# Moving the head norms, the ropes and the convolutions of a decoder layer in among the input projections

## The reference, cut to what matters

```python
h = _rmsnorm(x, P['norm1_w']) * (1.0 + sc1) + sh1
proj = jnp.einsum('btd,de->bte', h, P['w_in'])
q, kv, nsa_gate, dn_qkv, dn_a, dn_b, dn_z, merge = _split_cols(proj, IN_SPLITS)
q = _rope(_rmsnorm(q.reshape(B, T, NSA_HEADS, HEAD_DIM), P['q_norm_w']), pos)
kc = _rmsnorm(kc, P['k_norm_w'][0])
ksl = _rope(_rmsnorm(ksl, P['k_norm_w'][1]), pos)
kw = _rope(_rmsnorm(kw, P['k_norm_w'][2]), pos)
...
y = xx[:, 0:T] * P['dn_conv_w'][0]
for j in range(1, DN_CONV):
    y = y + xx[:, j:j + T] * P['dn_conv_w'][j]
y = jax.nn.silu(y)
```

## Time and profile before

| | us |
|---|---|
| median of 3 runs | 3313.51 |
| lowest and highest run | 3309.18 and 3320.33 |
| the profiled execution | 3319.12 |
| span of its trace | 3317.3 |
| TensorE busy | 2925.8 (88% of the span) |
| VectorE busy | 1695.2 (51%) |
| ScalarE busy | 965.3 (29%) |

### The profile page before, as it was taken

The page is one execution under the profiler, slowest core; times in us unless marked ns, Lnnn a source line. Parts: engine busy times, 40 slices in busy tenths (PEclk is TensorE's granted clock), DMA queues, the critical chain, the costliest instruction groups (busy, mean ns, idle before and its releaser), DMA issues.

```text
span 3317.3 us, 42568 instructions
## 1 busy us (share of the span) xinstructions
PE 2925.8 (88%) x16456; PEld 2463.2 (74%) x16456; DVE 1695.2 (51%) x2731; ACT 965.3 (29%) x1257; POOL 18.6 (1%) x21
## 2 busy tenths in 40 slices
PE   5799895684467879989889999999999999999999
PEld 2577773563256848879888888888887888888887
DVE  0154425551253150046535987777674666666665
ACT  1000001241121111123331135554443444444443
POOL 0000000000000000000000000000000000000000
PEclk8899997796678779989999999999999999999999
DMA  9565676113312036665433445566697788887885
GB/s 399 219 228 208 231 292 208 56 47 102 147 76 83 32 149 256 253 278 194 164 129 145 172 171 222 217 229 221 263 391 288 253 293 284 295 288 283 291 284 184
DMA packets 182494, 707.03 MB, mean 213 GB/s; under 512 B 20854, under 2 KB 119798, under 8 KB 144758
## 3 DMA queue, kind: packets, MB, share of 16 engines
q1 hardware_dynamic: 170726, 671.94, 54.7%
q10 hardware_dynamic: 9360, 16.85, 1.3%
q0 software_dynamic: 2304, 16.78, 1.3%
HBM read 662.81 MB, written 51.09 MB: 215 GB/s over the span
## 4 chain that ended last, share of the span: by engine, by line
PE 79%; DVE 10%; DMA 6%; SPq 2%; issue 2%; ACT 2%; DVEq 0%; ACTq 0%
PE psum L554 13%; PE psum L1039 12%; PE psum L1088 7%; PE psum L1090 7%; PE psum L1089 7%; PE psum L1040 6%; PE psum L998 5%; PE psum L914 3%; PE psum L915 3%; PE psum L916 3%; DMA ring<-in_w_ada 3%; PE psum L534 2%; PE psum L1019 2%; DMA ring<-in_w_in 1%; DVE xT L1572 1%
## 5 line engine op out<-in xcount | busy, mean ns | idle before, releaser
L554 PE MATMUL psum<-hT,ring 128*128 128x264 f32 x2560 | 602.4, 398 | 70.5 <-DMA ring<-in_w_in 33.6
L1995 DVE TENSOR_TENSOR w_lo<-ring,w_hi 128x1024 fp32r<-128x1024 f32 x464 | 545.0, 1219 | 196.5 <-ACT w_hi L1449 196.5
L554 PEld LDWEIGHTS psum<-hT,ring 128*128 128x128 f32 x2560 | 499.2, 196 | 168.8 <-issue 69.1
L1039 PE MATMUL psum<-h_both,w_hi 128*128 128x512 f32 x1664 | 593.1, 399 | 1.2 <-DVE h_both L2011 1.2
L1040 PE MATMUL psum<-h_both,w_lo 128*128 128x256 f32 x1664 | 466.0, 280 | 0.0
L1449 ACT ACTIVATE w_hi<-ring 128x1024 fp32r<-128x1024 f32 x464 | 451.9, 1045 | 32.8 <-ACT CK L1436 25.6
L1088 PE MATMUL psum<-w_hi,acts 128*128 128x512 f32 x1024 | 398.6, 389 | 0.5 <-DVE acts L2047 0.5
L1090 PE MATMUL psum<-w_hi,acts 128*128 128x512 f32 x1024 | 398.4, 389 | 0.0
L1089 PE MATMUL psum<-w_lo,acts 128*128 128x512 f32 x1024 | 398.4, 389 | 0.0
L1039 PEld LDWEIGHTS psum<-h_both,w_hi 128*128 128x128 f32 x1664 | 312.7, 188 | 79.4 <-issue 7.9
L1040 PEld LDWEIGHTS psum<-h_both,w_lo 128*128 128x128 f32 x1664 | 313.1, 188 | 0.0
(11 more groups left out here) (413 smaller groups left out, 3584.5 us busy)
## 6 DMA issues: line engine op xcount, KB each, us to landing
ring<-in_w_peer_u SPq DMA_DIRECT2D x64, 2048.0 KB, 8.7
ring<-in_w_peer_v SPq DMA_DIRECT2D x64, 2048.0 KB, 7.9
ring<-in_w_ada SPq DMA_DIRECT2D x48, 2048.0 KB, 12.2
ring<-in_w_in SPq DMA_DIRECT2D x42, 2048.0 KB, 8.0
arena<-gelu_scratch SPq DMA_DIRECT2D x64, 512.0 KB, 8.6
arena<-route_w SPq DMA_DIRECT2D x64, 512.0 KB, 9.4
ring<-in_cache_cmp SPq DMA_DIRECT2D x64, 256.0 KB, 3.4
ring<-in_cache_slc SPq DMA_DIRECT2D x64, 256.0 KB, 3.0
```

The costliest lines, as they stand in the source:

```text
L554: mm = pe.matmul(bank[b + j][:, 0:NT], w[:, k, j * P:(j + 1) * P], hT[:, k, :], start=(k == 0), stop=(k == KT - 1))
L1039: pe.matmul(out, top[:, k, c], h2_both[:, :, k, 0:SEQ], start=k == 0, stop=False)
L1995: dve.tensor_tensor(w_lo[:, s, cols], ring[:, s, cols], w_hi[:, s % 2, cols], ALU.subtract).then_inc(S["expert_lo"], 1)
```

## The change

The heads' norms and ropes and most convolutions are issued within the loops of stages 1 and 2, in places written out by hand; iterations 5 to 7 of stage 1 and all of stage 2 are unrolled for it. A place is 4 x iteration + j, where j is 0 and 1 ahead of the two tiles of slot 0 and 2 and 3 ahead of those of slot 2 on TensorE, and on VectorE the point behind each of the four big instructions of a cache's compression. The sums of squares of all 14 normed heads land in 14 rows of one bank (a one-column selector shifts each to its row); root and reciprocal are taken once, of 14x264; a product with a 14x128 selector spreads one row over 128 partitions again, and VectorE multiplies from PSUM. On VectorE `ada_bias` moves from ahead of the cache's compression to behind it. Constants grow by 27 columns. The other numbers of the head semaphores shift.

```diff
# TensorE
+            def head_sums():
+                pe.wait_ge(S["head_act"], 1)
+                for m in range(N_HEAD):
+                    mm = pe.matmul(bank[7][0:N_HEAD, 0:NT], cst("onecol")[:, 13 - m:13 - m + N_HEAD], hsq[:, m, :],
+                                   start=(m == 0), stop=(m == N_HEAD - 1))
+                mm.then_inc(S["head_pe"], 1)
+            def head_scales(n):
+                pe.wait_ge(S["head_dve"], n + 1)
+                for j in range(2):
+                    m = 2 * n + j
+                    mm = pe.matmul(bank[4 + 3 * j][:, 0:NT], ident[0:N_HEAD, m:m + 1].broadcast_to((N_HEAD, P)), hrow,
+                                   start=True, stop=True)
+                mm.then_inc(S["head_pe"], 1)
+            def head_turn(n):
+                pe.wait_ge(S["head_dve"], n + 8)
+                for j in range(2):
+                    mm = pe.matmul(bank[4 + 3 * j][:, 0:NT], cst("perm"), PR[:, ROPE_PAIRS[n] + j, :], start=True, stop=True)
+                mm.then_inc(S["head_pe"], 1)
+            def compressed_turn():
+                pe.wait_ge(S["head_dve"], 14)
+                pe.wait_ge(S["cmp_ready"], 1)
+                pe.wait_ge(S["ada_done"], 29)
...
+            def head_step(place):
+                if place == 5 * 4 + 1:
+                    head_sums()
+                if 6 * 4 <= place < 6 * 4 + 7:
+                    head_scales(place - 6 * 4)
+                if 7 * 4 + 3 <= place < 7 * 4 + 3 + 6:
+                    head_turn(place - 7 * 4 - 3)
+                if place == 10 * 4:
+                    compressed_turn()
...
+            for i in range(3):
+                first_part(i + 8, lambda j: head_step(4 * i + 32 + j))
+                if i == 2:
+                    pe.wait_ge(S["cmp_done"], 1)
                 ada_reduce(1, 2 * i + 24)
                 ada_main(3, i + 12, 8)
                 ada_reduce(3, 2 * i + 25)
...
# ScalarE
+            def convolved(n):
+                tiles = slice(T_DNQ + 4 * n, T_DNQ + 4 * n + 4)
+                act.wait_ge(S["proj_evac"], T_DNQ + 4 * n + 8)
...
+                for b in range(4):
+                    act.wait_ge(S["conv_done"], 4 * n + b + 1)
+                    act.activation(PR[:, T_DNQ + 4 * n + b, 0:SEQ], convt[:, b, 0:SEQ], ACT.Silu).then_inc(S["conv_silu"], 1)
...
+            first_part(5, head_root)
+            first_part(6)
+            first_part(7)
+            for i in range(3):
+                first_part(i + 8, lambda j: convolved(2 * i + j) if 2 * i + j < 5 else None)
                 ada_copy(3, i + 12)
...
# VectorE
-            with dve.Fori(0, 8) as i:
-                ada_bias(i + 16, 2 * i + 32)
+            def cache_part(i, beside=lambda j: None):
                 dve.wait_ge(cache_full[3], 16 * PAGES * (i + 1))
...
+                        beside(3)
+                ada_bias(i + 16, 2 * i + 32)
...
+            def head_pair(n):
+                t0, w = HEAD_PAIRS[n]
+                dve.wait_ge(S["head_pe"], n + 2)
+                for j in range(2):
+                    ins = dve.scalar_tensor_tensor(PR[:, t0 + j, :], PR[:, t0 + j, :], par("hw")[:, w:w + 1], bank[4 + 3 * j][:, 0:NT],
+                                                   ALU.mult, ALU.mult)
+                ins.then_inc(S["head_dve"], 1)
...
+            def head_step(place):
+                if place == 5 * 4 + 2:
+                    head_rows()
+                if 6 * 4 <= place < 6 * 4 + 7:
+                    head_pair(place - 6 * 4)
+                if 7 * 4 + 3 <= place < 7 * 4 + 3 + 6:
+                    rope_pair(place - 7 * 4 - 3)
...
+            with dve.Fori(0, 5) as i:
+                cache_part(i)
+            for i in range(5, 8):
+                cache_part(i, lambda j: head_step(4 * i + j))
+            for j in range(4):
+                convolve(2 * j)
+                convolve(2 * j + 1)
+                head_step(32 + j)
+            for m in (24, 25):
+                ada_bias(m, 2 * m)
+            head_step(36)
...
+            for t in range(8, 16):
+                convolve(t)
+            for m in (26, 27):
+                ada_bias(m, 2 * m)
...
+            for t in range(16, 20):
+                convolve(t)
+            for m in (28, 29):
+                ada_bias(m, 2 * m)
+            for t in range(20, DNT):
+                convolve(t)
# SyncE
-            sp.wait_ge(S["raw_saved"], 1)
-            sp.wait_ge(S["hist_new"], 1)
+            sp.wait_ge(S["raw_saved"], 6)
+            sp.wait_ge(S["hist_new"], 6)
```

More of the change, by code:

```diff
@@ L551, in project @@
                 for j in range(2):
+                    beside(j)
                     pe.wait_ge(S["proj_evac"], t + j + 1)
@@ new lines, in head_turn @@
+            def head_turn(n):
[7 more added lines that the diff above has]
+                pe.wait_ge(S["ada_done"], 29)
+                ck = CK[:, 0, :, :, 1:1 + N_CMP].rearrange("p b g n -> p (b g) n")
+                for m in range(2):
+                    pe.matmul(bank[4 + 3 * m][:, 0:8 * N_CMP], cst("perm"), ck[:, 8 * m:8 * m + 8, :], start=True, stop=True)
+                pe.matmul(bank[6][:, 64:64 + G * N_CMP_P], cst("perm"), CP[:, 0, :, :].rearrange("p g n -> p (g n)"),
+                          start=True, stop=True).then_inc(S["cmp_rot"], 1)
@@ L578, in _ @@
+            with pe.Fori(0, 5) as i:
+                first_part(i, lambda j: None)
                 ada_reduce(1, i + 16)
[L579 to L582, removed]
+            for i in range(5, 8):
+                first_part(i, lambda j: head_step(4 * i + j))
+                ada_reduce(1, i + 16)
+            for i in range(3):
+                first_part(i + 8, lambda j: head_step(4 * i + 32 + j))
+                if i == 2:
+                    pe.wait_ge(S["cmp_done"], 1)
@@ new lines, in _, with head_root @@
+            with act.Fori(0, 5) as i:
+                first_part(i)
+            act.wait_ge(S["proj_evac"], T_DNQ + 4)
+            for n, (t0, count) in enumerate(HEAD_GROUPS):
+                m = 0 if n == 0 else 6 + 2 * n
+                ins = act.activation(hsq[:, m:m + count, :], PR[:, t0:t0 + count, :], ACT.Square)
+            ins.then_inc(S["head_act"], 1)
+            def head_root(j):
+                if j == 0:
+                    act.wait_ge(S["head_pe"], 1)
+                    act.activation(hrow, bank[7][0:N_HEAD, 0:NT], ACT.Sqrt, bias=epst[0:N_HEAD, :],
+                                   scale=1.0 / P).then_inc(S["head_act"], 1)
@@ L1181, in _ @@
[L1181 to L1196, removed]
+            convolved(5)
             act.wait_ge(S["conv_done"], DNT + 1)
@@ L1595, in head_norm, with head_rows @@
                                          ALU.mult).then_inc(S["hn_done"], 1)
[L1597 to L1608, removed]
+            def head_rows():
+                dve.wait_ge(S["head_act"], 2)
+                dve.reciprocal(hrow, hrow).then_inc(S["head_dve"], 1)
@@ new lines, in head_pair, with rope_pair @@
+            def head_pair(n):
[5 more added lines that the diff above has]
+                ins.then_inc(S["head_dve"], 1)
+            def rope_pair(n):
+                t0 = ROPE_PAIRS[n]
+                x, t = PR[:, t0:t0 + 2, :], rtmp[:, 0:2, :]
+                dve.wait_ge(S["head_pe"], n + 9)
+                dve.wait_ge(S["head_dve"], n + 8)
+                for j in range(2):
+                    dve.tensor_tensor(t[:, j, :], bank[4 + 3 * j][:, 0:NT], cst("sin"), ALU.mult)
+                step(dve.tensor_tensor(x, x, cst("cos").unsqueeze(1).broadcast_to((P, 2, NT)), ALU.mult))
+                dve.tensor_tensor(x, x, t, ALU.add).then_inc(S["head_dve"], 1)
@@ L1610, in _ @@
+            with dve.Fori(0, 5) as i:
+                cache_part(i)
+            for i in range(5, 8):
+                cache_part(i, lambda j: head_step(4 * i + j))
[6 more added lines that the diff above has]
+            head_step(36)
+            dve.wait_ge(S["head_dve"], 14)
             for v, w in enumerate(("wck", "wcv")):
```

124 lines of the change are left out of this document (56 added, 68 removed).

## The result

The changed kernel takes **3240.06 us** (median of 4 runs, 3230.76 to 3246.44); beside it on the same chip the kernel before took 3312.71 (3309.18 to 3320.33). The ratio is 0.9774, with a 95% interval of 0.9752 to 0.9796: faster by 2.3%. The forecast was 3235, with a range of 3206 to 3265. The profiled execution took 3244.72 us, with a span of 3242.9.

The account below looks back on a forecast made before the run. TensorE was taken to bound stage 2, with stages 1, 3 and 4 bound by something else. Terms +8.3 + 5.7 - 63.0 - 29.7 = -78.7 us gave 3235 us for the median; 3206 to 3265 holds 8 in 10.

Parts of the forecast that it names:

- The moved `ada_bias`: Stage 1: compression starts when its pages land, w_in is no longer late, eight iterations of products take 247.2 us.
- rival B: Stage 1, iterations 0 to 4: w_in stays late behind the pages, 23.8 us more, 3259 us; chance 0.14.
- Head products: Stage 1 on TensorE: 14 sums 6.3, 14 spreads 6.3 and one turn 0.9, together 13.5 us.
- The new waits: Stage 1, places 25 and 29 (iterations 6 and 7): TensorE waits for VectorE's pair, 11.5 and 11.3 us.
- queue term: Stage 1: pages follow slot 2's load in SP's queue, 2.5 us per wait, 5.0 us in all.
- F: Stage 1: waits at places 25 and 29 don't arise, VectorE having pages earlier; 27.8 us less, 3207 us; chance 0.05.
- The slow starts: Stage 1: a slow first part on TensorE after each of the two waits, 2.5 us each, together 5.0.
- Stage 2: Five turns 4.5 us and the compressed turn 3.7, less a slow first part and its wait (2.5): +5.7 us.
- rival D: Lock-step: VectorE steps between places exceed TensorE's 8.1 us, each waits in turn; 93.5 us more, 3328 us; chance 0.03.
- Stages 3 and 4: Stage 3 goes but for the last `ada_reduce` and its `ada_bias`, 63.0 us off; z loses its wait, 29.7 off.
- rival E: z still stands still if the last convolutions end over 29 us into it: up to 26.1 us stay, 3261; chance 0.05.
- Rival C: Stage 1: pages wait for all of the load ahead in the queue, not half; 2 x 2.5 us more, 3240; chance 0.10.

Follow-up runs that it names:

- full-width reciprocals: Changed kernel with two unused 128 x 264 reciprocals added ahead of each head pair's multiplication on VectorE: 3248.04 us, ratio 0.9798.
- pages first: Changed kernel with SP issuing the eight cache pages ahead of slot 2's load instead of behind it: 3217.34 us, ratio 0.9716.
- second pair of single runs: Kernel before and changed kernel, both unchanged, each run once more for a second trace: 3311.9 and 3229.51 us.

## Why the prediction was right

The steps of the prediction were the right ones, and their sizes nearly so. That the sum of the stretch came out within 0.1 us, 461.8 for 461.7, is luck: stage 1 came out 1.9 us over, the rest 2.0 under, and within stage 1 larger errors cancel. By its own steps:

- **The moved `ada_bias`**: eight products' iterations at 30.9 us. Right: 30.99 in the changed kernel, and 247.8 us for the stage with the move alone, 247.2 forecast. SP's order did not keep slot 0's load late, so rival B falls; of its 23.8 us none is seen.
- **Head products**: 13.5 us forecast in stage 1, 14.8 measured. The sums cost 0.45 us each as assumed (from 293.63 to 299.97 is 6.34, for 14), but a spread of 14 rows 0.54 (1.08 for a pair): between the chosen 0.45 and the upper end of 0.6.
- **The new waits**: 11.5 and 11.3 us before the queue term, 14.0 and 13.8 with it; measured 12.52 and 11.80. Places and releaser were right: the second spread of iterations 6 and 7, waiting for VectorE's pair. That removes F (whose 27.8 us are the waits and only one of the two terms of 5.0 us that go with them; with both it would have been 3202). The queue term was mis-sized: from the first page's issue to the first product it took 14.4 us (325.22 to 339.58) and 13.8 in iteration 7 (377.04 to 390.88), against 13.4 with no load ahead (316.33 to 329.72), so 0.4 to 1.0 us for 2.5.
- **The slow starts**: 2.5 us each forecast from the one behind a wait of 6.9 us, where the granted clock is 0.85 over the slow slot; 3.6 measured behind 12 us, at 0.69, with the spread (1.0 longer) and the part (2.6 longer) both slow. The two waits came out 3.5 us under their forecast; the slow starts (2.2 over) and the head products (1.3 over) made that up, and smaller rests, 0.6 of them in the plain iterations, leave stage 1 at 1.9 us over.
- **Root and reciprocal**: one of 14 x 264 takes 1.79 us, as the 128 x 264 one of the earlier trace rows; it is hidden. That VectorE has room for far more was shown by the full-width reciprocals.
- **Stage 2**: 109.0 us for 110.3 forecast with the rest of stage 3. The compressed turn is 1.93 us long; I had taken 3.7 from a row behind an idle stretch and had named 1.9 as the other price. A place on VectorE was easier than assumed, since a convolution takes 1.8 us instead of 2.2. There was no lock-step, so rival D falls.
- **Stages 3 and 4**: z starts 0.27 us behind the last `ada_bias` and takes 57.3 us (58.0 forecast). ACT's first copy of z comes 10 us into it (13 forecast), far from the 29 that rival E wanted. With the convolutions late the same stall is back, so it was their place that made it.
- **SP's stores and pages**: the samples' pages were issued from 580.96 on, 45 us into z and not 35, and the first 16 were through by 598.2: the four stores ahead took SP 13 us instead of some 4, one of them (`p_conv`) 10.35. That cost nothing: the samples' attention begins only at 658.7, the end of the prompt's.

Rival C wanted the pages to wait for the whole load ahead of them. The profile's list of transfers around iteration 6, first of the changed kernel, then of the one with the pages first (the last number is the median time from issue to landing, in us):

```profile
ring<-in_w_in SPq DMA_DIRECT2D x1, 2048.0 KB, 9.0
ring<-in_cache_cmp SPq DMA_DIRECT2D x8, 256.0 KB, 5.8
```

```profile
ring<-in_cache_cmp SPq DMA_DIRECT2D x8, 256.0 KB, 3.5
ring<-in_w_in SPq DMA_DIRECT2D x1, 2048.0 KB, 8.4
```

A page does land 2.3 us later behind the load, in the median. But VectorE waits for the last of eight, and SP needs some 10 us to get from the first to that one, by which time the 9.0 us of the load are over. From the end of SP's issue to the first product it is 2.7 us in both iterations with the load ahead (325.22 + 11.66 = 336.88 to 339.58) and 3.0 without it (326.72 to 329.72), so nothing of the load is left to wait for; the 0.4 to 1.0 us lie in SP's issue itself, 11.66 and 11.13 us for 10.39. That removes C. The Trainium skill's rule of ring order ("DMA: Bandwidth & Descriptors", section "Queues, rings and completion order") is not contradicted by this. What a load ahead costs where its pages are issued faster than it is through, no run here shows.

The distance to the median came out less well: 72.7 us gained by the medians for 78.7 forecast. By the first traces the stretch gained 78.8, and the two attentions behind z gave 3.5 and 3.7 us back, of which the rest of the program regained some (the span shrank by 74.4). The prediction had put nothing there, and whether that part is the change's is open, as said above. The second pair of single runs has 82.4 (3311.9 - 3229.51). The runs of the changed kernel, 3230.76 to 3246.44, lie further apart than the 5 us by which the forecast missed.

## What to carry to other kernels

Work of one engine that bounds a stage can cost little beside a stage bound by another: 24 us of reciprocals, on the path in stage 3, cost 6 between the projections. It is not free: the head steps as built cost 47.6 us of stage 1, and 22.4 with the pages first (270.2 - 247.8). Before such work is put in order between matmuls, look at what its engine does just ahead of it: here a wait for cache pages, queued behind a weight load that nobody needed yet, cost 24 us of waits, and one swapped line in the load queue took 20 of them back. And undo the parts one by one: nearly half of this change was a single wait that stood ahead of work that did not need it.

## What was not expected of the hardware

- A convolution of four VectorE instructions took 2.2 us in a loop of before and 1.82 in plain code, with single instructions equally long (483 ns in both). In that loop ACT also loaded its table anew for each four Silus, 1.28 us each time; in plain code it loaded it once for all 24. Whether it is the loop itself or its addresses from registers was not separated.
- A pair of products whose contraction is 14 rows took 1.08 us, a pair of 128 rows (the turns) 0.89 to 0.99, with the same 264 columns. The single matmuls are equally long (381 and 386 ns), so fewer rows were no cheaper. Whether the longer pace comes from the rows or from the selector, one column repeated, was not separated.
- A reciprocal of 14 x 264 takes as long as one of 128 x 264 (1792 and 1777 ns), and one of 128 x 528 takes 3446: in these rows the columns count and the partitions do not.
- The same stretch of the same program took 58.5 or 65.5 us in two executions, at a granted clock of 0.97 and 0.85, with the same work ahead of it; what decides it is open.
